# A hybrid decoder trunk with routed experts: another order of the experts, a fifth slot for split weights, earlier reads of the lower results, and constant transposes in TensorE's waits

## The reference

```
xn      = rms_norm(x) * g
g_idx   = argmax(softmax(xn @ w_rg + b_rg))              # one of 4 groups for each token
e1, e2  = the two best experts of that group's 4 experts (16 in all)
gates   = softmax(logit e1, logit e2) * p_group
x      += sum over e in (e1, e2): gate_e * ((silu(xn @ w_g[e]) * (xn @ w_u[e])) @ w_d[e])
```

## The kernel before

| engine | step e before |
|---|---|
| TensorE | gate-up of expert e+1 (pairs 0 to 3, six matmuls each, the hidden rows of e transposed behind pair 1), 8 transposes of the gathered rows of e+2 (L624), down of e (pairs 4 and 5) |
| ScalarE | split of pair 3; copy of hidden e (L907); splits 4, 5; SiLU of e+1 (L888); two row copies of e+2 (L883); split 0 of the next; first down result (L922); split 1; second down result (L926); split 2 |
| VectorE | low half 3; hidden e (L965); 4, 5; product for e+1 (L944); two row halves of e+2 (L937); 0, 1, 2 of the next |
| GpSimd | gather e, scatter e-4, a part of the overflow's places, loads of the next layer's gains |

## Time and profile before

### The profile page before, as it was taken

How to read it: one execution, slowest core, us unless ns; L and a number is a source line. 1 busy time by engine, 2 the same in 40 slices (tenths; PEclk the granted TensorE clock), 3 DMA queues, 4 the chain that set the end, 5 groups by cost and what they waited for, 6 DMA issues and landing times.

```text
span 1556.6 us, 22096 instructions
## 1 busy us (share of the span) xinstructions
PE 1458.1 (94%) x7676; PEld 1128.2 (72%) x7676; DVE 935.9 (60%) x1824; ACT 866.0 (56%) x1668; POOL 457.7 (29%) x638
## 2 busy tenths in 40 slices
PE   7999999999999996999699999999999999889993
PEld 6887777677777785777578877766777777667772
DVE  3555654644554446999754565645454535579996
ACT  4456655555453335888554655555554433558883
POOL 3414318410000024873104152284000000268210
PEclk9999999999999997999899999999999999989997
DMA  7822222142232366999675222211422332669995
GB/s 178 141 79 63 60 63 64 53 109 68 62 115 75 105 204 215 353 358 351 242 198 112 79 58 60 68 55 55 109 68 61 115 101 92 232 218 371 369 347 209
DMA packets 155381, 231.01 MB, mean 148 GB/s; under 512 B 20579, under 2 KB 89955, under 8 KB 155268
## 3 DMA queue, kind: packets, MB, share of 16 engines
q1 hardware_dynamic: 143780, 209.62, 44.8%
q0 software_dynamic: 10768, 17.80, 3.5%
q10 hardware_dynamic: 720, 2.16, 0.4%
HBM read 220.99 MB, written 29.69 MB: 161 GB/s over the span
## 4 chain that ended last, share of the span: by engine, by line
PE 71%; DVE 12%; ACT 5%; issue 4%; POOL 4%; DMA 4%; SPq 0%; ACTq 0%; DVEq 0%; POOLq 0%
PE bank L528 19%; PE bank L530 17%; PE bank L529 17%; PE bank L1526 4%; DVE xT L593 4%; PE bank L1511 3%; PE bank L1502 3%; PE bank L1504 2%; ACT xT L587 2%; DVE oT L937 1%; DVE gate_t L1937 1%; DMA ac<-xn_dram,tab_i 1%; PE bank L1558 1%; DMA q_c<-ytok 1%; DMA raw<-in_w_in_dram 1%
## 5 line engine op out<-in xcount | busy, mean ns | idle before, releaser
L528 PE MATMUL bank<-wh,xT 128*128 128x512 f32 (+1 forms) x960 | 398.7, 415 | 8.0 <-DVE gate_t L1937 4.6
L530 PE MATMUL bank<-wh,xT 128*128 128x512 f32 (+1 forms) x960 | 373.7, 389 | 0.0
L529 PE MATMUL bank<-wl,xT 128*128 128x512 f32 (+1 forms) x960 | 372.8, 388 | 0.0
L474 ACT ACTIVATE wh<-raw,gcol 128x512 fp32r<-128x512 f32 (+1 forms) x208 | 148.7, 716 | 203.8 <-PE bank L530 195.8
L481 DVE SCALAR_TENSOR_TENSOR wl<-raw,gcol,wh 128x512 fp32r<-128x512 f32 (+1 forms) x208 | 162.5, 783 | 136.3 <-ACT wh L474 128.9
L528 PEld LDWEIGHTS bank<-wh,xT 128*128 128x128 f32 x960 | 180.5, 188 | 75.1 <-issue 23.0
L530 PEld LDWEIGHTS bank<-wh,xT 128*128 128x128 f32 x960 | 180.1, 188 | 37.5
L529 PEld LDWEIGHTS bank<-wl,xT 128*128 128x128 f32 x960 | 181.1, 189 | 29.9 <-issue 1.4
L1875 DVE CUSTOM_DVE_ANT_0 prob<-bank,mask 128x128 f32<-128x128 f32 (+3 forms) x128 | 60.6, 489 | 192.3 <-PE bank L1502 103.0
L2197 POOL TENSOR_TENSOR rows<-x_rows,ac 128x512 f32<-128x512 f32 x16 | 21.9, 1404 | 509.9 <-DVE x_rows L1946 509.9
L1664 ACT ACTIVATE prob<-prob,nmax 128x128 f32<-128x128 f32 (+3 forms) x192 | 107.2, 560 | 113.2 <-DVE nmax L1875 112.9
(11 more groups left out here) (339 smaller groups left out, 2697.6 us busy)
## 6 DMA issues: line engine op xcount, KB each, us to landing
raw<-in_w_in_dram SPq DMA_DIRECT2D x192, 256.0 KB, 2.7
bqkv<-in_w_expert_gate_dram SPq DMA_DIRECT2D x64, 256.0 KB, 5.1
bqkv<-in_w_expert_up_dram SPq DMA_DIRECT2D x64, 256.0 KB, 6.5
bqkv<-in_w_expert_down_dram SPq DMA_DIRECT2D x32, 512.0 KB, 7.7
q_c<-in_w_expert_gate_dram SPq DMA_DIRECT2D x64, 256.0 KB, 5.8
q_c<-in_w_expert_up_dram SPq DMA_DIRECT2D x64, 256.0 KB, 7.7
head_odd<-in_w_expert_down_dram SPq DMA_DIRECT2D x32, 512.0 KB, 7.7
raw<-in_w_branch_dram SPq DMA_DIRECT2D x48, 256.0 KB, 2.6
```

Of the source, the lines that this page charges most:

```text
L474: nc.scalar.activation(wh[:, i % HL, 0:width], raw[:, i % RAW, 0:width], ACT.Copy, scale=piece_gain(i))\
L528: nc.tensor.matmul(out, lhs[0], rhs[0], start=start, stop=False)
L529: nc.tensor.matmul(out, lhs[0], rhs[1], start=False, stop=False)
L530: return nc.tensor.matmul(out, lhs[1], rhs[0], start=False, stop=stop)
```

## The change

- `ORDER`: the experts are run in the order 0, 4, 8, 12, 1, 5, ..., 3, 7, 11, 15, so that of each group the fourth expert comes last. All block 0 results are then scattered after 12 experts (`LOW_DONE`).
- SP reads block 0 of tile 0 at step 14 and of tiles 1 to 3 at step 15, behind that step's weight loads; the destinations of the two blocks are swapped (block 0 into `rows`, block 1 into `q_c`). VectorE adds tile 0 in step 14 and tiles 1 to 3 behind step 15. Only block 1 is read behind the last scatter.
- The ring has a fifth slot, in `wh[:, 0:2]` and `wl[:, 0:2]`. Splits 4 and "0 of the next" move ahead in both queues.
- `gate_weights` is cut in two parts, at the head of VectorE's queue in steps 12 and 13.
- `keep_warm(spare, n)`: n transposes of the identity matrix into a bank that nobody reads: 30 before the mask matmuls, 10 before the rank's, 5 before the homes', 24 before the first rows' transposes, 8 behind them; 14 before each layer's x transposes, in layer 1 behind the landing of the last scatter.

```diff
+ORDER = [EG * (e % NG) + e // NG for e in range(NE)]
+LOW_DONE = NE - NG
...
+        def keep_warm(spare, n):
+            for _ in range(n):
+                nc.tensor.transpose(spare[:, 0:P], ident[:], ident[:])
...
         def pair_ring(e, j, par):
-            return j if is_const(e, -1) else (2 * par + j) % 4
+            return (0, 1, 4, 2, 3)[pair_no(e, j) % 5]
+        def pair_half(r, a):
+            return (wl if a else wh)[:, 0:2] if r == 4 else pair_w[:, r, a]
...
         def pair_hi(e, j, par, half):
-            if j >= 4:
-                pair_multiplied(nc.scalar, e, j - 4)
-            elif is_const(e, 0):
-                pair_multiplied(nc.scalar, -1, j)
-            elif not is_const(e, -1):
-                pair_multiplied(nc.scalar, e - 1, j + 2)
+            if is_const(e, -1):
+                if j == 2:
+                    multiplied(nc.scalar, END[GID["out", 1]])
+            elif j == 5:
+                pair_multiplied(nc.scalar, e, 0)
+            elif not is_const(e, 0):
+                pair_multiplied(nc.scalar, e - 1, j + 1)
+            elif j:
+                pair_multiplied(nc.scalar, -1, j - 1)
...
         def experts_sp(sp, layer):
+            def step_and_low(e, par, half):
+                step(e, par, half)
+                if e == NE - 2:
+                    sp.wait_ge(xn_out, of(xn_out, 16 * NT))
+                    for q in range(2):
+                        sp.wait_ge(y_out[q], of(y_out[q], 16 * LOW_DONE // 2))
+                    low_back(0)
+                if e == NE - 1:
+                    for n in range(1, NT):
+                        low_back(n)
...
         def experts_pe(pe):
+            keep_warm(h_bank[1], 30)
             pe.wait_ge(r_mask, of(r_mask, 1))
...
+            keep_warm(h_bank[1], 10)
             pe.wait_ge(r_ranked, of(r_ranked, 1))
...
+            keep_warm(h_bank[1], 5)
             pe.wait_ge(r_homed, of(r_homed, 1))
...
+            keep_warm(h_bank[1], 24)
             turn_chunk(0, 0, 0)
+            keep_warm(h_bank[1], 8)
             pe.wait_ge(xgT_lo, of(xgT_lo, 2))
...
         def experts_act(act, layer):
                 if not end:
                     pair_hi(e, 3, par, half)
+                    pair_hi(e, 4, par, half)
                 act.wait_ge(hid_turned, of(hid_turned, e + 1))
...
                 if not end:
-                    pair_hi(e, 4, par, half)
                     pair_hi(e, 5, par, half)
+                    pair_hi(e + 1, 0, 1 - par, half + par)
                     gate_silu(e + 1, 1 - par)
                     if not is_const(e, NE - 2):
                         rows_hi(e + 2, par)
-                    pair_hi(e + 1, 0, 1 - par, half + par)
...
         def experts_dve(dve, layer):
+                if e in (12, 13):
+                    gate_weights(dve, e - 12)
                 if not end:
                     pair_lo(e, 3, par, half)
+                    pair_lo(e, 4, par, half)
...
                 if not end:
-                    pair_lo(e, 4, par, half)
                     pair_lo(e, 5, par, half)
+                    pair_lo(e + 1, 0, 1 - par, half + par)
                     silu(e + 1, 1 - par)
-                    if not is_const(e, NE - 2):
+                    if is_const(e, NE - 2):
+                        add_first(0)
+                    else:
                         rows_lo(e + 2, par)
-                    pair_lo(e + 1, 0, 1 - par, half + par)
                     pair_lo(e + 1, 1, 1 - par, half + par)
...
-            gate_weights(dve)
+            for n in range(1, NT):
+                add_first(n)
...
             def tiles_turn(layer):
                 pe.wait_ge(ident_in, 16)
+                if layer:
+                    pe.wait_ge(y_out[1], of(y_out[1], 0))
+                keep_warm(acc[0], 14)
```

More of the change, by code:

```diff
@@ L788, in step, with low_back @@
                         passed(pair_no(e - 2, 4 + c) + 1)
-                        load_down(sp, layer * NE + e, c, par, pair_in[par][4 + c])
-            expert_steps(step)
+                        load_down(sp, layer * NE + ORDER[e], c, par, pair_in[par][4 + c])
+            def low_back(n):
+                sp.dma_start(back(n, 0), ytok_block(0, n)).then_inc(back_in[n], 16)
+            def step_and_low(e, par, half):
[8 more added lines that the diff above has]
+                        low_back(n)
+            expert_steps(step_and_low)
             passed(pair_no(NE - 2, 3) + 1)
-            sp.wait_ge(y_out[0], of(y_out[0], 16 * NE // 2))
-            sp.wait_ge(y_out[1], of(y_out[1], 16 * (NE // 2 - 1)))
-            for n in range(EARLY):
-                sp.dma_start(back(n, 0), ytok_block(0, n)).then_inc(back_in[n], 16)
             overflow_sp(sp, layer)
@@ L908, in step @@
                 if end and layer + 1 < DEPTH:
+                    pair_multiplied(act, NE - 2, 4)
                     now[0] = layer + 1
@@ L984, in experts_dve @@
                 now[0] = layer
-            for n in range(EARLY):
-                add_first(n)
             overflow_dve(dve)
             for n in range(NT):
-                if n >= EARLY:
-                    add_first(n)
                 add_last(n)
@@ L1017, in back @@
         def back(n, k):
-            return rows[:, n, :] if k else q_c.rearrange("p h s -> p (h s)")[:, n * D:(n + 1) * D]
+            return q_c.rearrange("p h s -> p (h s)")[:, n * D:(n + 1) * D] if k else rows[:, n, :]
         def experts_pool(pool, layer):
@@ L1029, in home @@
                     pool.wait_ge(y_zero, of(y_zero, 16))
-                scatter(ysb[:, e % 2, :], home_i[:, e:e + 1], y_out[e % 2])
+                scatter(ysb[:, e % 2, :], home_i[:, ORDER[e]:ORDER[e] + 1], y_out[e % 2])
             for e in range(NE):
@@ L1158, in overflow_slots, with gate_weights @@
                 chain(nc.vector.tensor_tensor(dst[:, NE:], marks[:, c, 0:n_ov], first_col, ALU.add))
-        def gate_weights(dve):
+        def gate_weights(dve, part):
             tt, ts = nc.vector.tensor_tensor, nc.vector.tensor_scalar
+            swap, keep = r1[:, 14, :], r1[:, 15, :]
+            if part:
+                chain(tt(r1[:, 25, :], r1[:, 23, :], r1[:, 5, :], ALU.mult))
+                chain(ts(keep, swap, -1.0, 1.0, ALU.mult, ALU.add))
+                for k in range(2):
+                    tt(r1[:, 28 + k, :], r1[:, 24 + k, :], keep, ALU.mult)
+                    chain(tt(r1[:, 30 + k, :], r1[:, 25 - k, :], swap, ALU.mult))
+                chain(tt(r1[:, 26:28, :], r1[:, 28:30, :], r1[:, 30:32, :], ALU.add))
+                return
             dve.wait_ge(r_act, of(r_act, 2))
@@ L1168, in gate_weights @@
             nc.vector.tensor_copy(r1[:, 24, :], r1[:, 23, :])
-            chain(tt(r1[:, 25, :], r1[:, 23, :], r1[:, 5, :], ALU.mult))
-            swap, keep = r1[:, 14, :], r1[:, 15, :]
-            chain(ts(keep, swap, -1.0, 1.0, ALU.mult, ALU.add))
-            for k in range(2):
-                tt(r1[:, 28 + k, :], r1[:, 24 + k, :], keep, ALU.mult)
-                chain(tt(r1[:, 30 + k, :], r1[:, 25 - k, :], swap, ALU.mult))
-            chain(tt(r1[:, 26:28, :], r1[:, 28:30, :], r1[:, 30:32, :], ALU.add))
         def place_overflow(pool, part):
```

27 lines of the change are left out of this document (11 added, 16 removed).

## The result

The changed kernel takes 1546.4 us (median of four runs, 1544.4 to 1547.1) beside 1560.0 (four runs, 1557.6 to 1564.2): ratio 0.9896, 95% interval 0.9878 to 0.9915, some 1.0% faster (it was 0.9890 in a later group, below). The profiled execution took 1545.84 us and spans 1544.0; its mean granted clock is 0.987, of before 0.974. The forecast was 1553, and -8.4 us between the profiles, which set 12.65 between them.

What follows compares the result with a forecast made beforehand. TensorE, 94% busy, was taken as the bound, with winnable waits in routing, behind the last expert and before pair 0. Terms -1.1 + 2.8 - 4.8 + 0.3 - 2.4 - 3.0 - 0.2 = -8.4 us gave 1553 us, range 1546 to 1559.

Steps and rivals of the forecast that it cites:

- Steps: Expert steps: fifth slot and new order move TensorE's wait to pair 1, step 9.88 to 9.85 us, -1.1 us in all.
- pair 1's loop: Expert step: pair 1's first matmul through down half, copy, split, VectorE's half, back to TensorE; claimed to set 9.85 us.
- to TensorE 1.37: Expert step: time from the start of VectorE's half to TensorE's matmul, 1.37 us, read at pair 0.
- 14 steps in each of two layers: Expert steps: number of steps claimed to get shorter, 28 in the bounds, for -1.1 us.
- Gate weights: Steps 12 and 13: the two parts delay VectorE's half of pair 3, costing 0.65 and 0.75 us, +2.8 us for two layers.
- The neighbouring row: Step 11: overflow slots in the same place, 0.78 us that cost 0.31, used to size the gate weights' delay.
- GpSimd: Layer 0: the tenth gather lands just when its transposes want it, so an earlier TensorE may wait; +0.3 us.
- Routing: Router to first expert: constant transposes keep TensorE's clock full, 2.4 us a layer allowing for falls in gaps, -4.8 us.
- Turnover and end: Behind the last expert: four reads and adds remain; -2.4 us in the turnover, -3.0 at the end, -0.2 for the scatter.
- The offset: Whole time: the median's 2.9 us above the profiled time, carried over from the kernel before to reach 1553 us.
- the wider one: Whole time: the prediction's outer range, 1546 to 1559 us.
- the rivals: Fifth slot frees step (0.10, 1542); clock not kept (0.18, 1558); constants delay work (0.06, 1568); weights or GpSimd bind (0.04, 1556).

Runs made afterwards that it cites:

- the kernel with late constants: Changed kernel with only the 24 constant transposes before the first rows' transposes and the 8 behind them, without the 30, 10, 5 and 14: 1549.7 us, ratio 0.9924.

## Why the forecast was off

**Steps (-1.1 forecast, -3.9 measured without the gate weights).** The mechanism was right: the wait moved from pair 0 to pair 1, and pair 1's loop sets the step. The step of the forecast that failed is a term of the sum, "to TensorE 1.37": a row for a matmul with three semaphores, put in for one with a single one, where it is 1.28. With it the step is 9.78, and 28 x 0.07 = 2.0 us. The run with three waits gives the forecast's 9.85 back. The second size that was off is the count, "14 steps in each of two layers": the last two steps gained 0.33 and 0.30 as well. Their kernel-before value, 14.9 us, stayed with constants alone, so it comes from the rest of the change; from which part, no run tells.

**Gate weights (+2.8 forecast, +2.5 measured).** 0.49 and 0.73 in layer 0, 0.50 and 0.75 in layer 1, where 0.65 and 0.75 were forecast. The neighbouring row was a good gauge.

**GpSimd (+0.3 forecast, 0 measured).** Steps 7 and 8 of layer 0 together took 0.31 more than plain ones in both kernels (0.7 and 0.5 in their second profiles). At 9.78 us the gather is nearly in time; at 9.55 it took 1.4 us back.

**Routing (-4.8 forecast, -5.4 measured).** 2.9 a layer was the bound, 2.4 was taken for a fall of the clock in a gap, and 2.7 came. Such falls occur, but cost little. In nine of the twenty routings the clock fell inside the 30 constants (5.16 to 5.43 us instead of 3.49), where they delay nobody; in six inside the 5 and the 24 (the 24 in 3.5 to 3.8 us instead of 2.8), and these still took 13.1 to 13.5 us to the second rows. What the forecast did not see is the late landing: two routings in twenty lose 2 us by it, 0.7 of them through the clock.

The rule of the Trainium skill (TensorE: Matmul & The Clock Gate, Part 4: PE-mode transpose), that full clock does not engage for transposes, is not borne out here: between 592.96 and 601.00 TensorE ran 39 transposes of constants and 24 small matmuls at a granted clock of 1.00, and without the transposes it was 0.50. By the rule the part would have won nothing, by the rows it won 5.4 us.

**Turnover and end (-5.6 with the last scatter, -5.6 between the first profiles, 8.5 to 8.8 by the other runs).** That sum and places agree between the first two profiles is luck. Between the second profiles of both kernels the turnover is 4.4 us shorter and the end 4.3, and putting the reads back cost 5.2 and 3.3. So the forecast's way of counting, adds and gaps alone, is the second step that failed. It kept the way from the last add to TensorE's tenth matmul the same; with four adds behind the scatter that was 4.92 us in nine of ten profiles and 5.27 in one, with the reads of before 4.93, 5.85, 5.94 and 6.64, the last three with the last tile's transposes at half clock. The rest lies in later landings and adds.

**The offset.** Of the 6.6 us between 1553 and 1546.4, 4.2 are the terms above and 2.4 the way from profile to median: the forecast carried over 2.9, and after the change it is 0.5. The short turnover and end of the first profile of before would account for that, but a median has no stages, so this is not shown. The forecast gave 0.46 to faster by over 0.5%, which came, and 0.49 to the same. The time lies under its own range of 1549 to 1557 and just inside the wider one; of the rivals none came, for no step is near 9.45 and routing won.

## What to carry to other kernels

When a loop's term is taken from a row, take it from an instruction with the same waits: a matmul that looks at three semaphores starts 0.1 us later than one that looks at one, and in a loop that is paid every time. A fifth buffer wins only what the order of instructions lets it: here ring and order won 0.11 us a step, one split moved ahead of one copy 0.20 more, and then, in layer 0, GpSimd's queue and the landing of the weights became the bound. Small work belongs into the wait that its own engine has in every step, not at the step's start; and an engine that stands idle at the end of a stage is no free place if a scatter is issued beside its work. Take a second profile before a stage's time goes into a sum: here the turnover and the end of the unchanged kernel differed by 2.0 and 1.2 us between two, and a stage that nothing touched by 1.7.

## What the runs showed of the hardware

- A waiting matmul with two more semaphores, both long set, starts 0.07 to 0.10 us later. The Trainium skill (Advanced Engine Details and Errata, Miscellaneous Facts) gives 50 to 100 ns for a sequencer's reading of a semaphore; for two that makes an estimate of 0.1 to 0.2 us, and the measured time lies at its lower end or under it.
- Constant transposes kept TensorE at 2.4 GHz through most of routing, where without them it ran at 1.2 (granted clock 1.00 from 587 to 607 beside 0.50 from 588 to 604), with at least one fall in 16 of 20 routings; 14 of them behind a wait of 4.51 us ran at 1.2 GHz to their end (3.22 us), as did the 16 real ones behind them (3.67).
- A stage of some 572 us that no edit touches took 1.4 to 1.8 us less in the four profiles of fourteen in which the clock did not fall behind a wait of 2.0 us in its middle.
- A scatter's issue on GpSimd took 0.97 us with VectorE idle, and 1.98 and 1.93 with adds beside all of it.
- The first gather of a layer is transposed 7.3 to 8.2 us behind the ranks' first matmul in 24 routings and 9.0 and 9.2 behind it in two. The two are in two kernels whose other routings are among the 24; the kernel with late constants, where the constants set it, is left out.
